# The first norm's root behind the first condition group, and nine early weight slots spread over condition slots 22 to 64, in a one-core decoder step

## The reference, cut to what matters

```
ada = jnp.dot(jax.nn.silu(c), p["w_ada"]) + p["b_ada"]
sh1, sc1, gt1, sh2, sc2, gt2 = jnp.split(ada[:, None, :], 6, axis=-1)
h = _rmsnorm(x, p["g_norm1"]) * (1.0 + sc1) + sh1
... = _split_cols(jnp.dot(h, p["w_in"]))
...
mix = (jax.nn.sigmoid(gate_gdn) * jnp.dot(o_gdn, p["w_gdn_out"]) + ...)
```

## Time and profile before

| what | value |
|---|---|
| median of 3 runs | 1912.66 us (1910.23 to 1913.7) |
| the profiled execution, its own time | 1912.93 us |
| its span | 1911.1 us |
| PE busy | 1848.5 us, 97% |
| POOL, ACT, DVE busy | 62%, 42%, 33% |
| DMA, mean | 205 GB/s |

### The profile page before, as it was taken

The page is one execution under the profiler, slowest core; times in us unless marked ns, Lnnn a source line. Parts: engine busy times, 40 slices in busy tenths (PEclk is TensorE's granted clock), DMA queues, the critical chain, the costliest instruction groups (busy, mean ns, idle before and its releaser), DMA issues.

```text
span 1911.1 us, 41519 instructions
## 1 busy us (share of the span) xinstructions
PE 1848.5 (97%) x16664; PEld 1742.3 (91%) x16664; DVE 632.5 (33%) x1792; ACT 809.7 (42%) x1372; POOL 1181.8 (62%) x508
## 2 busy tenths in 40 slices
PE   5899999999999999999999999999999999999997
PEld 2688999999888878888999999999999999999996
DVE  3224644444423341423433523221133231122333
ACT  3354445665323232323434655543344443344442
POOL 0356666666344334436876677777777777777773
PEclk9999999999999999999999999999999999999999
DMA  9967543443797878779764444444544444444452
GB/s 391 408 251 224 196 158 135 146 153 133 236 304 246 304 246 307 245 277 304 232 228 158 154 166 165 165 165 165 166 165 166 167 165 166 168 166 166 165 182 83
DMA packets 145661, 391.28 MB, mean 205 GB/s; under 512 B 27778, under 2 KB 36498, under 8 KB 144882
## 3 DMA queue, kind: packets, MB, share of 16 engines
q1 hardware_dynamic: 125536, 374.62, 56.9%
q10 hardware_dynamic: 19986, 14.70, 2.5%
HBM read 379.70 MB, written 8.88 MB: 203 GB/s over the span
## 4 chain that ended last, share of the span: by engine, by line
PE 88%; DVE 2%; SPq 2%; DMA 2%; issue 1%; POOL 1%; ACT 1%; DVEq 0%; ACTq 0%; POOLq 0%; PEldq 0%
PE bank L2440 26%; PE bank L2441 25%; PE bank L2445 25%; PE bank L2400 3%; DMA raw_c<-in_stream 1%; PE bank L2943 1%; DMA raw_a<-in_stream 1%; SPq L724 1%; PE bank L2389 1%; PE bank L2374 1%; POOL rest_a L850 0%; SPq L730 0%; PE bank L2828 0%; PE bank L2677 0%; SPq L702 0%
## 5 line engine op out<-in xcount | busy, mean ns | idle before, releaser
L850 POOL TENSOR_TENSOR rest_a<-raw_a,hi_a 128x1024 fp32r<-128x1024 f32 (+1 forms) x168 | 399.5, 2380 | 245.0 <-ACT hi_a L915 244.0
L2440 PE MATMUL bank<-h_hi,hi_a 128*128 128x288 f32 x1696 | 467.9, 302 | 4.8 <-ACT hi_a L915 2.3
L2441 PE MATMUL bank<-h_lo,hi_a 128*128 128x288 f32 x1696 | 458.6, 296 | 0.0
L2440 PEld LDWEIGHTS bank<-h_hi,hi_a 128*128 128x128 f32 x1696 | 320.5, 189 | 22.8 <-issue 16.1
L2441 PEld LDWEIGHTS bank<-h_lo,hi_a 128*128 128x128 f32 x1696 | 321.4, 190 | 0.2
L915 ACT ACTIVATE hi_a<-raw_a 128x1024 fp32r<-128x1024 f32 x165 | 174.6, 1059 | 283.9 <-PE bank L2445 198.1
L850 POOL TENSOR_TENSOR rest_b<-raw_b,hi_a 128x1024 fp32r<-128x1024 f32 x74 | 178.2, 2408 | 103.9 <-ACT hi_a L915 103.9
L2445 PE MATMUL bank<-h_hi,rest_a 128*128 128x288 f32 x1456 | 222.0, 295 | 1.4 <-POOL rest_a L850 1.3
L2445 PEld LDWEIGHTS bank<-h_hi,rest_a 128*128 128x128 f32 x1456 | 203.2, 188 | 1.9 <-POOL rest_a L850 1.9
L2440 PE MATMUL bank<-h_hi,hi_b 128*128 128x288 f32 x640 | 173.9, 298 | 0.0
L2441 PE MATMUL bank<-h_lo,hi_b 128*128 128x288 f32 x640 | 172.1, 295 | 0.0
(11 more groups left out here) (546 smaller groups left out, 3788.4 us busy)
## 6 DMA issues: line engine op xcount, KB each, us to landing
raw_a<-in_stream SPq DMA_DIRECT2D x364, 512.0 KB, 3.5
raw_b<-in_stream SPq DMA_DIRECT2D x179, 512.0 KB, 3.5
raw_c<-in_stream SPq DMA_DIRECT2D x94, 512.0 KB, 3.3
raw_m<-in_stream SPq DMA_DIRECT2D x27, 512.0 KB, 6.3
raw_e<-in_stream SPq DMA_DIRECT2D x12, 512.0 KB, 9.4
st<-in_state ACTq DMA_DIRECT2D x8, 512.0 KB, 6.2
st<-in_state SPq DMA_DIRECT2D x8, 512.0 KB, 6.6
out_state_s<-st ACTq DMA_DIRECT2D x8, 512.0 KB, 6.3
```

What stands on the lines that cost most here:

```text
L850: nc.gpsimd.tensor_tensor(rest_in(name, r)[:, :, cols], raw_of(name, r)[:, :, cols], w_hi[q].bitcast(f32)[:, :, cols], ALU.subtract).then_ ...
L2440: MM(banks[c][:, 0:N], w_, hi_of(k), start=(first and k == 0), stop=False)
L2441: ins = MM(banks[c][:, 0:N], w_, lo_of(k), start=False, stop=False)
```

## The change

The Ln table is loaded ahead of the squares (`early_ln`), and the waiting for the constants goes with it. The four `add_squares` follow the first group's bias on DVE, the four `first_sum` stand on PE behind condition slot 9, `scale_x` begins one group earlier, and `lo_pair(m)` is asked for at even n, in the step of the group that makes its scale. The table `EARLY_AT` moves early slots 0 to 7 to condition slots 22, 25, 28, 35, 38, 41, 51 and 56 (before: 28, 32, 36, 40, 44, 48, 56 and behind the last), and early 8 stays behind the last; `early(E_IN - 2)`, which was early 7, is no longer called there. On ACT the hi of early 1, 4, 7 and 9 stands one rounding pair earlier.

```
-EARLY_AT = {(7, 0): (0,), (8, 0): (1,), (9, 0): (2,), (10, 0): (3,), (11, 0): (4,), (12, 0): (5,), (14, 0): (6,), (15, 4): (7, 8)}
+EARLY_AT = {(5, 2): (0,), (6, 1): (1,), (7, 0): (2,), (8, 3): (3,), (9, 2): (4,), (10, 1): (5,), (12, 3): (6,), (14, 0): (7,), (15, 4): (8,)}
...
+            act.wait_ge(const_in, 48)
+            early_ln()
             for q in range(4):
                 square_quad(q)
-            act.wait_ge(const_in, 48)
             rms(0)
...
-                if n in (2, 3):
-                    add_squares(2 * n - 4)
-                    add_squares(2 * n - 3)
-                if n in (4, 5):
-                    if n == 4:
-                        dve.wait_ge(rs_ready, 1)
-                    scale_x(2 * n - 8)
-                    scale_x(2 * n - 7)
-                if n == 5 or n in (8, 12):
-                    samples(n // 4 - 1)
-                if n == 5:
+                if n == 1:
+                    for q in range(4):
+                        add_squares(q)
+                if n == 3:
+                    dve.wait_ge(rs_ready, 1)
+                    scale_x(0)
+                    scale_x(1)
+                if n == 4:
+                    samples(0)
                     lo_pair(0)
-                if n == 6:
                     lo_pair(1)
                     lo_samples(0)
-                if n >= 7 and n % 2:
-                    lo_pair((n - 3) // 2)
-                if n in (9, 13):
-                    lo_samples((n - 5) // 4)
+                    scale_x(2)
+                if n == 5:
+                    scale_x(3)
+                if n in (8, 12):
+                    samples(n // 4 - 1)
+                if n >= 6 and n % 2 == 0:
+                    lo_pair(n // 2 - 1)
+                    if n % 4 == 0:
+                        lo_samples(n // 4 - 1)
...
-                    if s_ == 3 and n in (2, 3):
-                        first_sum(2 * n - 4)
-                        first_sum(2 * n - 3)
-            early(E_IN - 2)
+                    if (n, s_) == (2, 1):
+                        for q in range(4):
+                            first_sum(q)
             turn(2 * KT // CT - 1)
```

More of the change, by code:

```diff
@@ L993, in _ @@
             hi("early", 0)
+            hi("early", 1)
             round_pair(2)
-            hi("early", 1)
             hi("early", 2)
@@ L999, in _ @@
             hi("early", 3)
+            hi("early", 4)
             round_pair(4)
-            hi("early", 4)
             hi("early", 5)
@@ L1005, in _ @@
             hi("early", 6)
+            hi("early", 7)
             round_pair(6)
-            for e in (7, 8, 9):
-                hi("early", e)
+            hi("early", 8)
+            hi("early", 9)
             round_pair(7)
```

## The result

The changed kernel takes **1920.76 us** (median of 6 runs, 1916.82 to 1923.07) against 1911.9 of the kernel before (6 runs beside them, 1910.23 to 1913.7): a ratio of 1.0043 (95% interval 1.0034 to 1.0053), 8.9 us slower. The forecast of no change was wrong, and the time lies above the range. The profiled execution took 1921.96 us, 9.0 more than the one before; its span is 1920.2 us.

What follows compares the result with a forecast made beforehand. Up to about 105 us the stream of 512 KB slots sets the time, then PE. Dry DMA +2.8, slot 63 +2.3, early 7 -5.1, rest -0.3 give -0.3; clock +1.2 makes +0.9: median 1913.5, range 1909 to 1917.5.

Steps and rivals of the forecast that it cites:

- The root: Norm's root on ACT: its Exp ends near 28.5 instead of 38.6 us; worth nothing by itself.
- The walk: PE's condition stage stepped through at 2.4 GHz: early 8 starts at 111.4 against 111.7, sum -0.3 us.
- forecast A: Condition stage: dry DMA queue and early 5's wait eat the tail's gain; 1910.5 to 1916.5, chance 0.71.
- the term *Clock: PE at 1.2 GHz behind waits ahead of early 3, 5 or 6: 1.2 us each, one taken, +1.2.
- the stated upper bound, +5.3: Clock cost on PE if early 3, 5, 6 and early 8 all run at 1.2 GHz: +5.3 us.
- Rival C: Waits ahead of early 3, 5 and 6 each hand PE back at 1.2 GHz: +5.0, 1918, chance 0.15.
- The dry queue: DMA engines stand 2.8 us because early 5's wait frees slot 49's buffer late; slot 63 lands at 107.9.
- The tail's gain: Early 7 moved off the tail: early 8 starts at about 106.9 if slot 63 stays on time, up to 4.8 us.
- All that follows shifts rigidly: Everything after early 8's start, projection loads and early 9 to 11 included, moves with that instant in both kernels.

Runs made afterwards that it cites:

- experiment 7: Changed kernel with unread matmuls only in PE's waits ahead of early 3, 5, 6 and turn 14: 1915.34 us, ratio 1.0017.
- 8: Changed kernel with early 3 to 6 put back to condition slots 36, 40, 44 and 52: 1915.32 us, ratio 1.0018.
- 12: Changed kernel, early 3 to 6 at slots 36, 40, 44, 52, early 5's hi before rounding pair 4, unread matmuls ahead of early 3, 6, turn 14: 1910.75 us.
- experiment 3: Changed kernel with the old table, early 7 back behind the last slot and the old order of hi on ACT: 1915.03 us, ratio 1.0013.
- Experiments 2: Changed kernel with unread matmuls behind most of condition slots 13 to 21 and ahead of early 3, 5, 6 and turn 14: 1913.16 us, ratio 1.0002.
- experiment 4: Kernel before with early 7 ahead of condition slot 60 instead of behind slot 63: 1910.38 us, ratio 0.9991.
- 6: Changed kernel with unread matmuls only behind condition slots 12 to 21, none in the waits: 1921.96 us, ratio 1.0048.
- experiment 9: Kernel before with unread matmuls between condition slots 13 and 28, ahead of early 4, behind slot 59, ahead of slots 62 and 63: 1913.78 us, ratio 0.9999.
- experiment 1: Changed kernel with early 5 ahead of condition slot 44 instead of slot 41: 1921.63 us, ratio 1.0040.

## Why the prediction was wrong

Medians beside their own runs of before: the changed kernel +8.9, the clock kept in the waits (experiment 7) +3.6, cover (8) +3.6, both with early 5's hi ahead (12) -1.7. At the projection start the last three are 4.7, 5.1 and 10.5 us earlier than the changed kernel. So about 5 us of the loss are the low clock, which experiment 7 removes by itself. The rest is PE's waiting for ACT and DVE. The forecast had foreseen these waits, and priced all that is not the clock some 2 us too low.

*The root* was right: its Exp ended at 28.15 (28.5 predicted), and by itself it gave nothing that can be told (experiment 3).

*The walk* against the trace of after:

| instant | walk | trace | lag |
|---|---|---|---|
| turn 7 | 60.1 | 60.86 | 0.8 |
| early 3 starts, ends | 64.7, 68.2 | 65.91, 70.78 | 1.2, 2.6 |
| early 5 starts, ends | 79.9, 83.4 | 82.43, 87.29 | 2.5, 3.9 |
| early 6 starts, ends | 93.0, 96.5 | 96.50, 101.37 | 3.5, 4.9 |
| early 7 ends | 103.2 | 107.85 | 4.7 |
| turn 14 | 108.0 | 112.79 | 4.8 |
| early 8 starts | 111.4 | 117.24 | 5.8 |

The events of forecast A are all there: early 5 waits 3.79 us for ACT's hi (3.8 predicted), turn 14 waits for DVE, the queue runs dry just before 90 us. Turn by turn the lag grows mainly where the clock is low: 1.4 us at each of early 3, 5 and 6, and 1.0 in the last slots (113.89: 1.95 us for two slots, which take 1.05 at the higher clock, and the turn of 1.02 behind them). The 0.8 up to turn 7 may be early 0's low clock (43.15 to 47.51); no run took that away. Another 0.4 comes between turn 7 and early 3 at the higher clock, and 0.6 is caught up in between.

**The step that failed is the term *Clock*: "I take one, +1.2".** PE was at the lower clock under all three of early 3, 5 and 6 (1.4 us each over the walk), in the last slots (1.0) and under early 8 (117.24 to 121.96, 4.7 us instead of 3.4, 1.3): 6.5 us in place of 1.2. That the whole lag at the projection start is 6.5 as well is chance. Taken away in experiment 7, these stretches gave back 4.7 us there and 5.3 in the median, less than 6.5, since PE then waits 1.12 and 0.46 us for data. Even the stated upper bound, +5.3, left out the condition slots behind turn 14. Rival C, with a chance of 0.15, was the mechanism as far as the clock goes; its 1918 was too low. The reasoning that went astray was that a wait of 1.95 us had cost no clock at 76.88 in the earlier trace rows: it was a sample of one, with full work ahead of it, and I gave the waits of 2.7 to 3.8 us, which resembled the costly ones at 41.67 and 101.41, the benefit of it.

The Trainium skill, "TensorE: Matmul & The Clock Gate", section "Loop structure matters more than you think", has matmuls back to back as its good case and a long wait for DMA between them as its bad one. Carried over to these waits for ACT, as the prediction did, it has all three places low, +3.6. The trace of after agrees on all three (4.9 us each).

Experiments 2 and 7 show a remedy: matmuls in the wait.

**The dry queue was mis-sized too, 2.8 us against 6.6 measured, but these are not further microseconds.** The walk was on time to within a microsecond until turn 7. From there PE's lag went into the queue: the walk has early 5's end at 83.4, the trace at 87.29, so the refill was 3.9 us later, and 2.8 + 3.9 = 6.7. The lateness of PE came first, and in the changed kernel no slot behind slot 34 waits for its data. The queue matters only once PE is faster: in experiment 7, at the higher clock, the shares still miss 4.5 us (0.89, 0.51, 0.75 of 1.02), PE waits 1.6 us for data, and slot 63 lands at 111.25, where the walk had it land at 107.9 and run near 110. Forecast A without its clock term was -0.3; the projection start in experiment 7 says +1.8. So 3.5 us of the miss at the projection start are the clock term (4.7 against 1.2) and 2.1 the others.

*The tail's gain* of up to 4.8 was right in kind. Experiment 12 has early 8 at 107.03, where the term had put it. In the changed kernel early 8 was also predicted to run at 2.4 GHz behind the turn; it ran at 1.2.

**What stays open.** "All that follows shifts rigidly" can't be tested to better than some microseconds. From the first projection slot to the end all these kernels run the same instructions, and the profiled executions took 1786.1 us for it before, 1788.7 in the changed kernel, 1783.9 in experiment 3 and 1793.0 in experiment 4, with the other ten in between; the lag at the start of it and its length show no clear relation. So of the 9 us, 6.5 are there at the projection start, and the other 2.6 are within what this part scatters by. What makes it scatter no run here was aimed at. For the same reason a gain of 4.0 us at the projection start (experiment 12) is not yet a gain in the time.

## What to carry to other kernels

Count the clock as a cost of every wait of the engine that heads the chain, not only the idle time: here each wait of 2.7 to 3.8 us costs about another 1.4 in the early slot behind it. A DMA queue that runs dry behind a late engine is first of all that lateness seen from another place: look for the engine's wait for data before counting it as a cost of its own. Before spreading work ahead to fill an engine, write down for each piece what makes its operand and what covers that chain; a piece directly behind the turn that its chain starts from has no cover. Filling an unavoidable wait with matmuls that nobody reads can return more than it costs, but only where the engine's lag is what the end hangs on (experiment 7, not 6), and where they don't make the loads late themselves (experiment 9).

## What the runs showed of the hardware that was not expected

- The clock can fall after PE has resumed: early 5 began with matmuls of 0.37, 0.29 and 0.29 us and went on at 0.44 from the fifth, under work without a break. A long wait is paid for later than it is seen.
- Waits of the same length can leave either clock. Behind 1.95 us early 4 took 3.5 us in the earlier trace rows; behind 1.87 us in experiment 3 and 1.90 in experiment 4 an early slot took 4.9. Behind 2.38 us early 5 took 4.9 in experiment 1 (82.20 to 87.07) and 3.5 in experiment 8 (82.00 to 85.52). Wherever PE stood idle for 2.6 us or more ahead of an early slot, the slot was at the lower one.
- The low stretch ahead of early 0 can be shortened (35:40 from 0.50 to 1.00, 40:45 to 0.67) without any effect on the projection start (experiment 6: 131.52), since PE waits for data there. Early 0 itself still took 4.2 us against 4.4, so its own low clock wasn't tested.
